# Attention layer of a two-layer encoder: low parts of the turned tiles on VectorE, mixing operations spread, both row maxima in one reduction, lambda's sums earlier

## The reference

```python
def diff_attention(h, cos, sin, w_qkv, w_o, q_gain, k_gain, lam_q1, lam_k1, lam_q2, lam_k2, sub_gain, lambda_init):
    qkv = h @ w_qkv                                   # h (1, 512, 1024), 8 heads, two maps of 64 per head, V of 128
    q = partial_rope(rmsnorm(q, q_gain), cos, sin)    # per head and map
    k = partial_rope(rmsnorm(k, k_gain), cos, sin)
    lam = exp(sum(lam_q1 * lam_k1)) - exp(sum(lam_q2 * lam_k2)) + lambda_init
    s = einsum('mbhqd,mbhkd->mbhqk', q_blk, k) / sqrt(64)
    p = softmax(s, axis=-1)
    o = einsum('bhqk,bhkv->bhqv', p[0] - lam * p[1], v)
    o = rmsnorm(o, sub_gain) * (1.0 - lambda_init)
    return o @ w_o

def reference(x, ...):                                # all float32
    for i in range(2):                                # layer 0: diff_attention, layer 1: multiscale_pool
        x = x + mixer(rmsnorm(x, norm_mix[i]))
        x = x + square(relu(rmsnorm(x, norm_mlp[i]) @ w1[i])) @ w2[i]      # 1024 -> 4096 -> 1024
    return x
```

## Time and profile before

| | |
|---|---|
| median of 3 runs | 1030.07 us (1029.33 to 1031.6) |
| the profiled execution | 1029.67 us, span 1027.9 us |
| granted TensorE clock | 0.990 |
| PE busy | 984.7 us (96%), weight loads 807.5 |
| DVE busy | 861.0 us (84%) |
| ACT busy | 485.0 us (47%) |
| POOL busy | 427.7 us (42%) |

### The profile page before, as it was taken

The page is one execution under the profiler, slowest core; times in us unless marked ns, Lnnn a source line. Parts: engine busy times, 40 slices in busy tenths (PEclk is TensorE's granted clock), DMA queues, the critical chain, the costliest instruction groups (busy, mean ns, idle before and its releaser), DMA issues.

```text
span 1027.9 us, 12963 instructions
## 1 busy us (share of the span) xinstructions
PE 984.7 (96%) x4724; PEld 807.5 (79%) x4724; DVE 861.0 (84%) x1123; ACT 485.0 (47%) x743; POOL 427.7 (42%) x371
## 2 busy tenths in 40 slices
PE   5999998889899899999999999999999999999998
PEld 4877776666678688888888888898888888888887
DVE  5567889877955999999999987777998999899883
ACT  4525655577745524434345353355443443443520
POOL 5852687565556273664860400252404304124000
PEclk9999999999999999999999999989999999999999
DMA  6423211220123233323332333301333333332202
GB/s 245 143 49 103 62 42 41 65 100 1 49 73 126 82 103 112 111 86 116 90 120 86 102 104 122 119 5 62 103 102 103 103 102 107 102 112 90 70 14 82
DMA packets 52047, 92.76 MB, mean 90 GB/s; under 512 B 8848, under 2 KB 9872, under 8 KB 51984
## 3 DMA queue, kind: packets, MB, share of 16 engines
q1 hardware_dynamic: 45888, 91.24, 27.9%
q10 hardware_dynamic: 6096, 0.69, 0.5%
HBM read 89.82 MB, written 2.10 MB: 89 GB/s over the span
## 4 chain that ended last, share of the span: by engine, by line
PE 76%; DVE 13%; POOL 4%; issue 3%; ACT 2%; DMA 1%; ACTq 1%; SPq 0%; DVEq 0%; POOLq 0%
PE bank L1602 73%; DVE s_nmax L1263 2%; PE bank L1660 2%; DVE s_w_lo L1153 1%; POOL s_o_r L703 1%; DVE s_p L1285 1%; POOL s_oc L706 1%; DVE s_mixc L1283 1%; DVE s_qkn L1215 1%; DVE s_hT_lo L1336 1%; DMA s_raw<-in_attn_w_qkv 1%; DVE s_rt L1219 1%; DVE s_o_ss L1312 1%; DVE s_qk_ss L1202 1%; DVE s_oc L1273 1%
## 5 line engine op out<-in xcount | busy, mean ns | idle before, releaser
L1602 PE MATMUL bank<-s_hT_hi,s_w_hi 128*128 128x512 f32 x512 | 200.8, 392 | 0.0
L1602 PE MATMUL bank<-s_hT_hi,s_w_lo 128*128 128x512 f32 x512 | 199.3, 389 | 0.0
L1602 PE MATMUL bank<-s_hT_lo,s_w_hi 128*128 128x512 f32 x512 | 199.3, 389 | 0.0
L1153 DVE TENSOR_TENSOR s_w_lo<-s_raw,s_w_hi 128x1024 fp32r<-128x1024 f32 x96 | 155.9, 1642 | 13.9 <-ACT s_w_hi L819 7.7
L754 POOL TENSOR_TENSOR s_lt<-s_lbB,s_lbB 128x1024 f32<-128x1024 f32 x14 | 34.1, 2439 | 268.7 <-PE bank L1602 268.2
L1173 DVE TENSOR_TENSOR s_lbB_lo<-s_lbB,s_b_hi 128x1024 fp32r<-128x1024 f32 x64 | 122.6, 1940 | 0.0
L1390 DVE TENSOR_TENSOR s_acc<-s_acc,bank 128x512 f32<-128x512 f32 x168 | 109.3, 681 | 11.0 <-PE bank L1602 10.8
L1602 PE MATMUL bank<-s_b_hi,s_u_hi 128*128 128x512 f32 x288 | 113.2, 393 | 1.9 <-DVE s_a_lo L1378 1.9
L1602 PEld LDWEIGHTS bank<-s_hT_hi,s_w_hi 128*128 128x128 f32 x512 | 96.2, 188 | 20.1 <-issue 0.5
L1602 PEld LDWEIGHTS bank<-s_hT_lo,s_w_hi 128*128 128x128 f32 x512 | 96.2, 188 | 20.0 <-issue 0.5
L1602 PEld LDWEIGHTS bank<-s_hT_hi,s_w_lo 128*128 128x128 f32 x512 | 96.1, 188 | 20.0
(11 more groups left out here) (197 smaller groups left out, 2189.8 us busy)
## 6 DMA issues: line engine op xcount, KB each, us to landing
s_raw<-in_mlp_w SPq DMA_DIRECT2D x64, 512.0 KB, 3.7
s_lbB<-in_mlp_w SPq DMA_DIRECT2D x64, 512.0 KB, 3.3
s_raw<-in_attn_w_qkv SPq DMA_DIRECT2D x24, 512.0 KB, 4.2
s_raw<-in_attn_w_o SPq DMA_DIRECT2D x8, 512.0 KB, 3.2
s_x_nat<-in_x SPq DMA_DIRECT2D x4, 512.0 KB, 8.5
s_x_again<-in_x SPq DMA_DIRECT2D x4, 512.0 KB, 5.0
out<-s_acc SPq DMA_DIRECT2D x8, 256.0 KB, 2.0
s_raw<-in_pool_w SPq DMA_DIRECT2D x4, 256.0 KB, 2.7
```

What stands on the lines that cost most here:

```text
L1153: v.tensor_tensor(w_lo[slot][:, cols], raw[k][:], f32(w_hi[slot][:, cols]), ALU.subtract)\
L1602: return nc.tensor.matmul(o, lhsT, rhs, start=start, stop=stop, **kw)
```

## The change

- `turn_lo` moves from GpSimd to VectorE and takes the unrounded value from bank 4 itself; ScalarE's second copy and the buffer `turn_raw` are gone. TensorE's `turn` waits for `turn_lo_done` in place of `turn_kept`. On VectorE the low part of a q, k or head stands first in the next iteration, the map's between `maxima` and `combine`.
- Two neighbouring banks are one tensor, and one reduction takes both maxima.
- `combine` is taken apart: the reciprocal of the second map's sum before `maxima`, the factor after it, the mix last. The map sums `lsum` are kept for all steps, and the head's statistics use the first map's sum in place of its reciprocal, with EPS multiplied by its square; the product `o_rl` on GpSimd is gone.
- Lambda's sums stand after slab 1's splits; the splits of slab 2 go one per tile into the loop over slab 1's tiles, on ScalarE and VectorE.
- In a step without fillers `values` comes before the extra turn.

```diff
@@ GpSimd
-            def turn_lo(what, n):
-                k = TURN_NO[what, n]
-                hi, lo = turn_dst(what, n)
-                pool.wait_ge(turn_kept, k + 1)
-                g.tensor_tensor(lo, turn_raw[:, k % 2, :], f32(hi), ALU.subtract).then_inc(turn_lo_done, 1)
...
-                    link(g.tensor_tensor(o_rl[:], o_r[:], rl0[:, NT * h:NT * h + NT], ALU.mult))
                     o_tile = oc[:, h % 2, :].rearrange("p (t d) -> p t d", t=NT)
-                    g.tensor_tensor(o_tile, o_tile, o_rl[:].unsqueeze(2).to_broadcast([P, NT, VD]), ALU.mult)\
+                    g.tensor_tensor(o_tile, o_tile, o_r[:].unsqueeze(2).to_broadcast([P, NT, VD]), ALU.mult)\
                         .then_inc(o_normed, 1)
@@ ScalarE
-                a.activation(hi, bank[4][:], ACT.Copy, scale=scale)
-                if k >= 2:
-                    act.wait_ge(turn_lo_done, k - 1)
-                a.activation(turn_raw[:, k % 2, :], bank[4][:], ACT.Copy, scale=scale).then_inc(turn_kept, 1)
+                elif what in "qk" and n >= 2:
+                    act.wait_ge(scored, NT * (n - 1))
+                a.activation(hi, bank[4][:], ACT.Copy, scale=turn_scale(what)).then_inc(turn_kept, 1)
...
-                    if s == 2:
-                        split_hi(3, t, 1)
+                    if s:
+                        split_hi(s + 1, t, (s + 1) % 2)
...
                 if s == 0:
-                    for t in range(4):
-                        split_hi(2, t, 0)
                     act.wait_ge(lam_exp, 1)
@@ VectorE
+            def turn_lo(what, n):
+
+                k = TURN_NO[what, n]
+                hi, lo = turn_dst(what, n)
+                dve.wait_ge(turn_kept, k + 1)
+                if what == "map":
+                    last = v.tensor_tensor(lo, bank[4][:], f32(hi), ALU.subtract)
+                else:
+                    last = v.scalar_tensor_tensor(lo, bank[4][:], turn_scale(what), f32(hi), ALU.mult, ALU.subtract)
+                last.then_inc(turn_lo_done, 1)
+
             for t in range(NT):
                 split_lo(1, t, 1)
+            dve.wait_ge(lam_loaded, 16 * 4)
+            lam_sum = [v.tensor_tensor_reduce(out=lam_t[:, n, :], in0=lam_in[:, 2 * n, :],
...
+            lam_sum[1].then_inc(lam_exp, 1)
...
-                for m in range(2):
-                    last = v.tensor_reduce(nmax[:, i % 2, m:m + 1], bank[2 * (i % 2) + m][:], AX.X, ALU.max,
-                                           negate=True)
-                last.then_inc(max_done, 1)
+                v.tensor_reduce(nmax[:, i % 2, :], pair[i % 2][:], AX.X, ALU.max, negate=True).then_inc(max_done, 1)
...
+            def mix_root(i):
+
+                dve.wait_ge(exp_done, 2 * i + 2)
+                v.reciprocal(rl1[:, i % 2:i % 2 + 1], lsum[:, i, 1:2]).then_inc(mix_rooted, 1)
+
+            def mix_factor(i):
+
+                dve.wait_ge(mix_rooted, i + 1)
+                v.scalar_tensor_tensor(mixc[:, i % 2, :], lsum[:, i, 0:1], neg_lam[:, 0:1], rl1[:, i % 2:i % 2 + 1],
+                                       ALU.mult, ALU.mult).then_inc(mix_known, 1)
...
-                dve.wait_ge(exp_done, 2 * i + 2)
-                link(v.reciprocal(rl[:, q, :], lsum[:, q, :]))
-                v.tensor_copy(rl0[:, i:i + 1], rl[:, q, 0:1])
-                link(v.scalar_tensor_tensor(mixc[:, q, :], lsum[:, q, 0:1], neg_lam[:, 0:1], rl[:, q, 1:2],
-                                            ALU.mult, ALU.mult))
+                dve.wait_ge(mix_known, i + 1)
...
             for i in range(LAST + 1):
+                if i - 1 in EXTRA:
+                    turn_lo(*EXTRA[i - 1])
...
+                if 1 <= i <= STEPS:
+                    mix_root(i - 1)
                 if i < STEPS:
                     maxima(i)
                 if 1 <= i <= STEPS:
+                    mix_factor(i - 1)
+                if 2 <= i < STEPS + 2:
+                    turn_lo("map", i - 2)
+                if 1 <= i <= STEPS:
                     combine(i - 1)
...
-                    mine = rl0[:, NT * h:NT * h + NT]
-                    link(v.tensor_tensor(o_sq[:], mine, mine, ALU.mult))
+                    mine = lsum[:, NT * h:NT * h + NT, 0]
+                    v.scalar_tensor_tensor(o_sq[:], mine, EPS, mine, ALU.mult, ALU.mult)
                     dve.wait_ge(o_squared, h + 1)
                     link(v.tensor_reduce(o_ss[:], osq[:].rearrange("p (t d) -> p t d", t=NT), AX.X, ALU.add))
-                    link(v.tensor_tensor(o_sq[:], o_ss[:], o_sq[:], ALU.mult))
...
-                    v.tensor_scalar(o_v[:], o_sq[:], 1.0 / VD, EPS, ALU.mult, ALU.add).then_inc(o_v_done, 1)
+                    v.scalar_tensor_tensor(o_v[:], o_ss[:], 1.0 / VD, o_sq[:], ALU.mult, ALU.add).then_inc(o_v_done, 1)
@@ TensorE
                 if k:
-                    pe.wait_ge(turn_kept, k)
+                    pe.wait_ge(turn_lo_done, k)
...
+                values_first = not now and 3 <= i < STEPS
+                if values_first:
+                    values(i - 3)
                 if i in EXTRA and i < STEPS:
                     turn(*EXTRA[i])
-                if 3 <= i < STEPS + 3:
+                if 3 <= i < STEPS + 3 and not values_first:
                     values(i - 3)
```

More of the change, by code:

```diff
@@ L338, in build_trunk @@
         assert cursor[0] <= nc.sbuf_usable_end, (cursor[0], nc.sbuf_usable_end)
-        bank = [ctx.enter_context(nc.psum_tensor(f"bank{k}", [P, BANK], F32)) for k in range(8)]
+        pair = [ctx.enter_context(nc.psum_tensor(f"pair{k}", [P, 2, BANK], F32)) for k in range(2)]
+        bank = [pair[k // 2][:, k % 2, :] for k in range(4)]
+        bank += [ctx.enter_context(nc.psum_tensor(f"bank{k}", [P, BANK], F32)) for k in range(4, 8)]
         x_loaded = [sem(f"x_loaded{k}") for k in range(NT)]
@@ L381, in build_trunk @@
         exp_done = sem("exp_done")
+        mix_rooted = sem("mix_rooted")
+        mix_known = sem("mix_known")
         a_done = sem("a_done")
@@ L463, in turn_dst, with turn_scale @@
             return qkT_hi[n % 2][:, "qk".index(what), :], qkT_lo[n % 2][:, "qk".index(what), :]
+        def turn_scale(what):
+            if what == "map":
+                return 1.0
+            if what == "o":
+                return sub_col[:, 0:1]
+            return qk_col[:, 0:1] if what == "q" else qk_col[:, 1:2]
         def piece(slab, k):
@@ L1229, in v_lo_part @@
                     .then_inc(v_lo_done, 1)
+            def turn_lo(what, n):
+                k = TURN_NO[what, n]
+                hi, lo = turn_dst(what, n)
+                dve.wait_ge(turn_kept, k + 1)
+                if what == "map":
+                    last = v.tensor_tensor(lo, bank[4][:], f32(hi), ALU.subtract)
+                else:
+                    last = v.scalar_tensor_tensor(lo, bank[4][:], turn_scale(what), f32(hi), ALU.mult, ALU.subtract)
+                last.then_inc(turn_lo_done, 1)
             for t in range(NT):
                 split_lo(1, t, 1)
+            dve.wait_ge(lam_loaded, 16 * 4)
+            lam_sum = [v.tensor_tensor_reduce(out=lam_t[:, n, :], in0=lam_in[:, 2 * n, :],
+                                              in1=lam_in[:, 2 * n + 1, :], scale=1.0, scalar=0.0,
+                                              op0=ALU.mult, op1=ALU.add,
+                                              accum_out=lam_e[:, 2 + n:3 + n]) for n in range(2)]
+            lam_sum[1].then_inc(lam_exp, 1)
             for s in range(AHEAD):
@@ L1241, in _ @@
                         qk_norm(n - 1)
-                    if s == 0:
-                        split_lo(2, t, 0)
                     if n >= 2 * NT:
                         v_lo_part(0, t, bank[n % 4])
-                if s == 0:
-                    dve.wait_ge(lam_loaded, 16 * 4)
-                    lam_sum = [v.tensor_tensor_reduce(out=lam_t[:, n, :], in0=lam_in[:, 2 * n, :],
-                                                      in1=lam_in[:, 2 * n + 1, :], scale=1.0, scalar=0.0,
-                                                      op0=ALU.mult, op1=ALU.add,
-                                                      accum_out=lam_e[:, 2 + n:3 + n]) for n in range(2)]
-                    lam_sum[1].then_inc(lam_exp, 1)
+                    if n == 2 * NT + 1:
+                        turn_lo("q", 0)
+                    if n == 2 * NT + 2:
+                        turn_lo("k", 0)
                 if s == 1:
```

31 lines of the change are left out of this document (8 added, 23 removed).

## The result

The changed kernel takes 1017.44 us in the median (1016.6 to 1019.61, 4 runs) against 1029.99 of the kernel before beside it (1029.33 to 1031.6): ratio 0.9882, 95% interval 0.9864 to 0.99. That is 12.6 us less, at 1016.0 forecast. The granted clock is 0.993 (0.990), and the load fell on every engine: VectorE 855.7 us (861.0), ScalarE 457.4 (485.0), GpSimd 346.7 (427.7).

What follows compares the result with a forecast made beforehand. TensorE's waits in the attention (21.3 us from 88 to 320 us) and the slow clock were taken as the budget there. With the projections' gain the terms summed to -13.7: 1029.7 - 13.7 = 1016.0 us, range 1009 to 1026.

Steps and rivals of the forecast that it cites:

- Lambda and the splits: Projections: moving lambda's sums and slab 2's splits gains 3.7 us (1.8 waiting, 1.7 clock, 0.2 restart); bounds 1.8 to 4.0.
- the last comes at about 57: Projections: slab 2's splits, one per tile, are wanted at 60.6 us and the last comes at about 57.
- The term for the clock, 1.7: Projections, 62 to 76 us: the slow clock, 0.88 over 14 us, comes back, worth 1.7 us.
- Low parts and stretching: Attention: 34 us more VectorE work, against 0 to 28 us of stretching by GpSimd coming back, taken as 22.
- Mixing: Attention, VectorE: spreading the mixing operations saves 0.3 us a step, 10 us in all; lower bound 0.15 a step.
- Bank 4: Attention: TensorE's turns wait for VectorE's low parts, 5.2 us from 140 to 196 us and 2.4 from 196 to 306.
- a sign of being wrong: Attention: TensorE waiting 10 us or more for low parts at its turns would show the prediction wrong.
- By stretch: Projections -3.7 us; 88 to 140 us -0.3; 140 to 196 -3.5; 196 to 306 -5.5; the last head -0.7.
- A: Rival: only the projections gain, bank-4 stalls eating the head chain's gain: 1025 to 1027 us; chance 0.21 including ground from 1022.
- B: Rival: VectorE's stretching stays in the attention, each iteration 0.7 us longer, bank 4 sets the pace: near 1034 us; chance 0.08.
- C: Rival: all 5.6 us of attention clock loss and V's whole wait come back, another 5 us: 1006 to 1011; chance 0.12.
- D: Rival: no effect, only if the projections' wait returns elsewhere and A holds; chance 0.04.

Runs made afterwards that it cites:

- split_old_place: The changed kernel with slab 2's splits back in the loop over slab 0's tiles, lambda's sums still early: 1014.90 us.
- low_parts_only: The kernel before with only the low parts moved from GpSimd to VectorE, ScalarE copying once: 1030.64 us.
- collide: The changed kernel with an unused 512-column subtraction per turn put back on GpSimd where its low parts stood: 1024.93 us.
- spread_only: The kernel before with only reciprocal, factor and mix spread apart, two maxima and old statistics kept, one small reciprocal added: 1026.97 us.
- M: The mixing part (spread mixing, one reduction for both maxima, shorter head statistics); alone in the kernel before: 1024.59 us.
- L: The low-parts part (low parts moved from GpSimd to VectorE); alone in the kernel before it is low_parts_only: 1030.64 us.
- second_copy: The changed kernel with ScalarE copying bank 4 a second time, VectorE subtracting from that copy and TensorE waiting for the copy: 1012.40 us.
- early_low: The changed kernel with q, k and head low parts ahead of the same iteration's weight split in eight steps from 2 to 13: 1012.93 us.
- low_and_projections: The kernel before with low parts on VectorE and the lambda and split moves, without the mixing part: 1018.80 us.

## Why the prediction was right, point by point

**Lambda and the splits: right in kind, 2.9 in place of 3.7.** ScalarE takes the exponential at 41.57, issues its nine DMAs and goes on at 46.05, hidden as forecast. The 1.80 us wait is gone, and the clock from 62 to 76 us is 1.00. The term was too large because of "the last comes at about 57": I had followed ScalarE's half of slab 2's splits. VectorE does one norm and one split per tile, 3.83 us, in a row. VectorE's and TensorE's timelines after:

```profile
57.01 1.22 DVE L1140 TENSOR_TENSOR s_w_lo<-s_raw,s_w_hi 128x1024 fp32r<-128x1024 f32 x1
...
60.83 1.22 DVE L1140 TENSOR_TENSOR s_w_lo<-s_raw,s_w_hi 128x1024 fp32r<-128x1024 f32 x1
...
64.66 1.22 DVE L1140 TENSOR_TENSOR s_w_lo<-s_raw,s_w_hi 128x1024 fp32r<-128x1024 f32 x1
```
```profile
65.93 0.50 PE L1611 MATMUL pair<-s_w_hi,s_hT_hi 128*128 128x512 f32 x1 [0.79 <-DVE s_w_lo L1140]
```

The last low part comes at 64.66, and TensorE waits 0.79 us for it, about the 0.8 that the term had too much. By split_old_place the early sums are worth 4.2 us (52.57 - 48.34), and the spread splits take 1.3 back, of which this wait is 0.79. The term for the clock, 1.7, holds in the kernel before (0.90 and 0.76 from 60 to 70 us, behind the 1.80), but not as a rule: in low_parts_only TensorE waits 2.12 us at the same place, and the clock stays at 1.00.

**Low parts and stretching: the size held, the partner was missed.** The 22 to 26 us of stretching are gone with the low parts alone: 32 x (1.243 - 0.751) + 32 x (0.534 - 0.223) = 25.7. That one engine waited for the other is borne out by collide, where the factor ends with GpSimd's subtraction. What the prediction did not see is that this part needs the one about lambda: alone it gave no time. The prediction asked what hides the moved splits, and not who would now wait for VectorE at the turns of the first q and k. That costs 4.8 us where lambda's sums stay late.

**Mixing: 0.31 a step for the spread, as forecast.** The Trainium skill (VectorE: DVE Perf Modes, "The DRAIN you can't avoid") has a semaphore after each operation cost nothing extra, measured there on a chain of copies. The trace here does not agree: an operation that waits for the one right before it starts 0.18 us behind it, another 0.07, a cost of some 0.11 each. And spread_only, with as many operations as before, is 3.0 us faster, in part because the mix is stretched less (1026 ns on average against 1243). One reduction lasts 1206 ns, near the 1.2 assumed. VectorE's busy time in the attention (88 to 300 us before, 84 to 290 after) goes from 173.2 to 166.4, where -2 was forecast (the 211 us that the prediction sets beside it are in no row). The spread also moves the mix off GpSimd's subtraction (its mean falls from 1243 to 1005 with M alone, while the factor's rises from 534 to 595). This relief was booked under the low parts only, and L and M share it. They also share the wait for the head, 7.7 us before: 3.9 with L, 2.2 with M, 1.0 with both. These two are why their gains do not add, as far as the traces show; no run separates them.

**Bank 4: the place right, the sum too small.** Steps 10, 11, 14 and 6 stall 1.61, 1.89, 1.09 and 0.46 (forecast 1.7, 1.7, 0.9, 0.9). All together it is 11.3 us, forecast 7.6, and over the 10 that the prediction itself had named as a sign of being wrong. This is the term that it mis-sized most. Step 2 adds 0.77, the steps from 15 on have 3.7 (forecast 2.4), and the largest miss is step 8, where it is the map's low part that is late. VectorE's and TensorE's timelines:

```profile
135.72 1.56 DVE L1202 TENSOR_TENSOR s_qkn<-s_qs,s_qk_r 128x512 f32<-128x512 f32 x1
...
138.37 2.06 DVE L1140 TENSOR_TENSOR s_w_lo<-s_raw,s_w_hi 128x1024 fp32r<-128x1024 f32 x1
...
141.68 0.68 DVE L1224 TENSOR_TENSOR s_aT_lo<-bank,s_aT_hi 128x512 fp32r<-128x512 f32 x1
```
```profile
142.50 0.63 PE L1669 MATMUL bank<-s_ident,s_oc 128*128 128x128 f32 x4 [1.77 <-DVE s_aT_lo L1224]
```

The map was turned at 137.33, and its low part lies behind a norm and a split stretched by 0.88 and 0.84 us (0.68 and 1.22 elsewhere). GpSimd's square of a tile (135.69, 1.04 us) and its product for the head (138.22, 1.13) run beside them. That is 1.7 us in one iteration, where 0.5 was set down for collisions in the whole stretch. Only head and q, k turns were checked for lateness, not the map's. Behind this wait and the one of step 11 the clock falls (the figure behind the five busy times):

```profile
140.00:145.00 5.00, 3.23 (x19) 2.60 (x18) 4.97 (x10) 3.28 (x7) 1.10 (x1) 0.87 0.30 105
145.00:150.00 5.00, 5.00 (x23) 3.56 (x22) 1.94 (x4) 0.46 (x2) 2.44 (x2) 0.79 0.27 105
160.00:165.00 5.00, 3.11 (x22) 2.56 (x21) 4.83 (x12) 0.81 (x2) 2.92 (x2) 0.91 0.15 49
165.00:170.00 5.00, 5.00 (x22) 4.11 (x21) 4.86 (x11) 3.45 (x7) 2.91 (x3) 0.74 0.14 56
```

**By stretch.** Projections -2.45 (-3.7). From there to the start of step 8 (138.19 before, 136.43 after) +0.7 (-0.3), with the stalls of steps 2 and 6. Steps 8 to 14 -3.9 (-3.5): the extra stalls, and the 1.7 of clock that did not come back, are made up by V's wait, gone whole and not by half. From step 15 to the last head's turn -5.8 (-5.5 and a part of the last head's -0.7). Behind it about -1.1, which the prediction costed at nothing; what follows the last head's turn takes from 720.3 to 722.7 us in the kernels' profiled executions, and why stays open. The errors of 1 to 4 us in the terms cancel. The mechanisms held, but that their sum lands 1.4 us from the forecast is luck in part: bank 4 came out 3.7 too small, and the shared gain of L and M was not seen.

**Rivals.** A (1025 to 1027) falls: the heads' wait is under 3 us as said, at 1.0. B falls (VectorE's stretching went), but collide shows its mechanism: with the stretching back, 7.5 us are lost. C was half there: the clock loss came back in the last stretch and not in the third. Its time, 1006 to 1011 (of which only 1011 follows from "another 5 us"), is met only by a further edit: bank 4 freed by the copy gives 1012.4, with the old place 1010.2. D falls with A.

## What to carry to other kernels

Where work moves to another engine, look at who now waits for that engine in every stage, the first included, and for every kind of item that it handles; a hole that nobody noticed (7.1 us here) becomes a wait (3.84). Two edits that relieve the same collision don't add, and two of which one makes room for the other add more than their sum, so test them in pairs. When a slower engine's queue frees a buffer, a cheap copy by an idle one may pay for itself: here the wait fell from 11.3 to 2.8 us, and the clock in that stretch rose from 0.94 to 0.97.

## What the runs showed of the hardware

A 128x512 subtraction on GpSimd stretches VectorE's mix, which reads SBUF, whether or not anyone needs its result: medians of 744 ns with none and 977 with idle ones. What reads PSUM was not stretched. In collide the map's 32 low parts last 677 to 692 ns, also where GpSimd works beside them (161.69 for 0.68, GpSimd busy from 161.71); in second_copy, where they read SBUF, one lasts 1537 (213.08, beside GpSimd's product from 213.01 to 214.07). So moving an operand from SBUF to PSUM took VectorE's new work out of GpSimd's way.

The granted clock did not follow the length of a wait alone. In the changed kernel it fell to 0.79 from 145 to 150 us behind a wait of 1.77; in early_low TensorE waited 1.81 us at the same place, and the clock stayed at 1.00:

```profile
145.00:150.00 5.00, 5.00 (x27) 3.66 (x26) 3.69 (x8) 2.04 (x5) 1.18 (x2) 1.00 0.30 105
```

low_parts_only and low_and_projections, with nearly the same waits in the attention, also differ in it. Part of the scatter of a few us between executions of one kernel may lie there; what sets it was not settled.
